# Forget attention and the last attention turn four slabs of their output in their last places instead of two, and forget attention's scores rotate over three PSUM banks

## The reference, cut to what matters

```python
def even_layer(...):
    proj = rms_norm(h, norm_g) @ w_in
    ...
    oa = rms_norm(diff_attention(...), subln_g) * (1.0 - lam_init)        # 4 heads of 128: columns 0 to 511
    ob = fox_attention(qb, kb, vb, cum_logf)                              # 4 heads of 128: columns 512 to 1023
    mixed = concatenate([oa, ob], axis=-1) * silu(z)
    return h + mixed @ w_out

def odd_layer(...):
    ...                                                                    # 8 heads of 128, three dilated windows merged
    mixed = o.reshape(b, s_len, MIX_WIDTH) * silu(z)
    return h + mixed @ w_out
```

## Time and profile before

| | |
|---|---|
| runs of the kernel before | 1555.58, 1555.17, 1554.95 us; median 1555.17 |
| the profiled execution | 1554.78 us, its span 1553.0 us |
| TensorE busy | 1487.5 us, 96% of the span |
| VectorE, ScalarE, GpSimd busy | 850.9, 677.9 and 592.3 us |
| mean granted TensorE clock | 0.998 |

### The profile page before, as it was taken

How to read it: one execution, slowest core, us unless ns; L and a number is a source line. 1 busy time by engine, 2 the same in 40 slices (tenths; PEclk the granted TensorE clock), 3 DMA queues, 4 the chain that set the end, 5 groups by cost and what they waited for, 6 DMA issues and landing times.

```text
span 1553.0 us, 25078 instructions
## 1 busy us (share of the span) xinstructions
PE 1487.5 (96%) x9488; PEld 1240.5 (80%) x9488; DVE 850.9 (55%) x1879; ACT 677.9 (44%) x1377; POOL 592.3 (38%) x349
## 2 busy tenths in 40 slices
PE   4999998898999999999899999999999999999998
PEld 3778787787888878888788889967788788877887
DVE  4573708876764265933742997056322599617322
ACT  3333336565566353335744333467323433346332
POOL 1212223691005553447725444423234444430244
PEclk9999999999999999999999999999999999999999
DMA  9657620000012333331013323300233233310322
GB/s 326 181 140 192 175 62 27 2 2 1 2 35 89 108 109 96 95 95 42 28 33 94 96 82 98 93 14 28 69 93 106 75 99 101 96 41 1 109 82 95
DMA packets 103717, 128.61 MB, mean 83 GB/s; under 512 B 10608, under 2 KB 63792, under 8 KB 103600
## 3 DMA queue, kind: packets, MB, share of 16 engines
q1 hardware_dynamic: 103600, 127.01, 27.4%
HBM read 124.90 MB, written 2.10 MB: 82 GB/s over the span
## 4 chain that ended last, share of the span: by engine, by line
PE 81%; DVE 7%; POOL 5%; ACT 3%; issue 3%; DMA 1%; SPq 1%; DVEq 0%; ACTq 0%; POOLq 0%
PE psum L1048 21%; PE psum L1050 20%; PE psum L1049 20%; PE psum L1293 3%; PE psum L1236 3%; PE psum L1004 2%; PE psum L1215 2%; PE psum L1151 1%; PE psum L1340 1%; PE psum L1322 1%; PE psum L1272 1%; POOL rx L2403 1%; POOL mla_q L2403 1%; DVE psum L1943 1%; PE psum L1273 1%
## 5 line engine op out<-in xcount | busy, mean ns | idle before, releaser
L2353 POOL TENSOR_TENSOR wlo<-wraw,whi 128x1024 fp32r<-128x1024 f32 (+4 forms) x181 | 413.1, 2283 | 704.6 <-ACT whi L1445 704.6
L1445 ACT ACTIVATE whi<-wraw 128x1024 fp32r<-128x1024 f32 (+4 forms) x181 | 181.6, 1003 | 421.7 <-PE psum L1050 415.4
L1048 PE MATMUL psum<-whi,h2h 128*128 128x512 f32 (+2 forms) x800 | 309.5, 387 | 2.6 <-DVE h2l L1959 1.5
L1050 PE MATMUL psum<-whi,h2l 128*128 128x512 f32 (+2 forms) x800 | 305.2, 382 | 0.0
L1049 PE MATMUL psum<-wlo,h2h 128*128 128x512 f32 (+2 forms) x800 | 304.6, 381 | 0.0
L1048 PEld LDWEIGHTS psum<-whi,h2h 128*128 128x128 f32 x800 | 150.3, 188 | 28.5 <-issue 2.7
L1050 PEld LDWEIGHTS psum<-whi,h2l 128*128 128x128 f32 x800 | 150.2, 188 | 27.1
L1049 PEld LDWEIGHTS psum<-wlo,h2h 128*128 128x128 f32 x800 | 150.4, 188 | 24.8
L1048 PE MATMUL psum<-whi,hTh 128*128 128x512 f32 (+2 forms) x372 | 143.4, 385 | 3.7 <-DVE hTl L1959 2.7
L1050 PE MATMUL psum<-whi,hTl 128*128 128x512 f32 (+2 forms) x372 | 136.2, 366 | 0.0
L1049 PE MATMUL psum<-wlo,hTh 128*128 128x512 f32 (+2 forms) x372 | 135.8, 365 | 0.0
(11 more groups left out here) (391 smaller groups left out, 2956.4 us busy)
## 6 DMA issues: line engine op xcount, KB each, us to landing
rx<-mod_w_in SPq DMA_DIRECT2D x32, 512.0 KB, 5.1
wraw<-w_in_odd_in SPq DMA_DIRECT2D x32, 512.0 KB, 3.6
wraw<-cd_w_in_in SPq DMA_DIRECT2D x24, 512.0 KB, 3.7
wraw<-w_in_even_in SPq DMA_DIRECT2D x20, 512.0 KB, 3.7
wraw<-ab_w_out_in SPq DMA_DIRECT2D x16, 512.0 KB, 3.7
wraw<-w_ple_gate_in SPq DMA_DIRECT2D x16, 512.0 KB, 3.8
mod_w_even<-mod_w_in SPq DMA_DIRECT2D x8, 512.0 KB, 10.3
wraw<-ab_w_in_in SPq DMA_DIRECT2D x8, 512.0 KB, 8.3
```

What stands on the lines that cost most here:

```text
L1048: eng.matmul(dst, a[0], ww[0], start=first, stop=False)
L1050: mm = eng.matmul(dst, a[1], ww[0], start=False, stop=last_)
L1445: eng.activation(hi_of(u)[:, :, 0:w], wraw[:, u["id"] % RAW, :, 0:w], ACT.Copy).then_inc(*to("split_hi", u["id"]))
L2353: eng.tensor_tensor(lo_of(u)[:, :, 0:w], wraw[:, u["id"] % RAW, :, 0:w], f32(hi_of(u)[:, :, 0:w]), ALU.subtract)\
```

## The change

Five edits:

- `late_turn` turns slabs 0 to 3, in places 27 to 30 of the pair pipeline and in places 27 to 30 of the odd attention. It was slabs 0 and 1 in the last two of these.
- `turns_at` turns slabs 4 and 5 beside unit 0 of `out3` and `out4` and slabs 6 and 7 beside unit 1. It was 2 and 3, 4 and 5, 6 and 7 beside units 0, 1 and 2.
- The four early slabs go through bank 7.
- Fox keeps its probabilities in slabs 4 to 7 of `both_low` (which lies over `h2l`), not 2 to 5, so that the low parts of slabs 2 and 3 can be written.
- Fox's scores go into banks 0, 2, 3 by n mod 3. Diff keeps its banks: its last place, 15, uses banks 2 and 3. Fox's first place, 16, now uses bank 2 (16 mod 3 = 1), place 17 bank 3, place 18 bank 0.

```diff
-        for name, t_ in (("in2", "h2"), ("out3", "m3"), ("out4", "m4")):
-            for u in range(-1 if t_[0] == "h" else 0, 3):
-                turns_at[name, 0, u] = [(t_, 2 * u + 2, 2 * u + 4, XT) if t_ == "h2" else (t_, 2 * u + 2, 2 * u + 4)]
+        for u in range(-1, 3):
+            turns_at["in2", 0, u] = [("h2", 2 * u + 2, 2 * u + 4, XT)]
+        for name, t_ in (("out3", "m3"), ("out4", "m4")):
+            for u in range(2):
+                turns_at[name, 0, u] = [(t_, 2 * u + 4, 2 * u + 6)]
...
-        late_turns = {"fox": "m3", "odd": "m4"}
+        late_turns, EARLY_SLABS = {"fox": "m3", "odd": "m4"}, 4
...
-            groups = groups_of(late_turns[name], 0, 2)
+            groups = groups_of(late_turns[name], 0, EARLY_SLABS)
             n_ = j - (len(units_of(name)) - 1 - len(groups))
...
-                    if name[0] == "m" and k < 2:
+                    if name[0] == "m" and k < EARLY_SLABS:
                         bank_of[name, k, g[0]] = 7
...
             if PAIR[n_][0] == "fox":
-                return both_low[:, 2 + n_ % 4, a:b]
+                return both_low[:, 4 + n_ % 4, a:b]
...
+        def pair_scores(n_):
+
+            return 2 * (n_ % 2) if PAIR[n_][0] == "diff" else (0, 2, 3)[n_ % 3]
...
-                        s0, cols = score_bank(n_), slice(t * P, (t + 1) * P)
+                        s0, cols = pair_scores(n_), slice(t * P, (t + 1) * P)
```

More of the change, by code:

```diff
@@ L1687, in pair_attention @@
                             eng.wait_ge(*at("nmax", (name, j, m)))
-                            eng.activation(pair_probs(n_, m, 0, w), psum[:, score_bank(n_) + m, 0:w], ACT.Exp, bias=nmax[:, c_:c_ + 1], scale=-1.0,
+                            eng.activation(pair_probs(n_, m, 0, w), psum[:, pair_scores(n_) + m, 0:w], ACT.Exp, bias=nmax[:, c_:c_ + 1], scale=-1.0,
                                            accum_out=rsum[:, c_:c_ + 1]).then_inc(*to("exps", (name, j, m)))
@@ L2044, in pair_attention @@
                         for m in range(2 if name == "diff" else 1):
-                            c_, sc = pair_column(n_, m), psum[:, score_bank(n_) + m, 0:w]
+                            c_, sc = pair_column(n_, m), psum[:, pair_scores(n_) + m, 0:w]
                             eng.wait_ge(*at("scores", (name, j, m)))
```

## The result

| | before | changed |
|---|---|---|
| median | 1555.11 us (6 runs, 1554.83 to 1555.97) | 1560.51 us (6 runs, 1558.31 to 1561.49) |
| the traced execution | 1554.78 us, span 1553.0 | 1559.28 us, span 1557.5 |

The ratio of the means is 1.0032, 95% interval 1.0019 to 1.0045: slower by 0.3%. The changed kernel also scatters more: its six runs span 3.2 us, those of before 1.1. The mean granted clock of its runs is 0.995 to 0.999.

The account below looks back on a forecast made before the run. TensorE, busy 1487.5 of 1553.0 us, was taken as the bound. Fox and `out3` summed to +2.04, odd and `out4` to +0.81: +2.85, 1557.63 for a profiled execution, median 0.39 higher, so 1558.0 us; range 1554.6 to 1560.2.

Parts of the forecast that it names:

- stall at place 16: Start of fox: scores now in bank 2 wait for place 15's first softmax, starting 1060.69 instead of 1058.64: +2.05 us.
- clock behind it: Rival: after 3.0 us idle at place 16 the granted clock drops to 1.2 GHz, 1.7 us more; chance 0.20.
- place 24: Fox: the scores' wait for place 22's exponential goes, because of the third bank: -0.74 us.
- wait for the norm: Fox, place 27: slab 0's turning waits for GpSimd's last norm, which moves with the stall at place 16: +1.77 us.
- `out3`, unit 1: `out3`: unit 1 no longer waits for slab 3's low part, and no successor to the stall is found: -1.50 us.
- turnings in fox, with the two moved out of `out3`: Fox: a 0.24 us wait for bank 7, plus 0.22 for two slabs turned in attention: together +0.46.
- odd and `out4`: Odd attention: 0.22 us for two moved turnings and 0.59 for waits on bank 7, `out4` unchanged: +0.81 us.
- The clock falls at the seam: Rival, diff to fox at place 16: clock falls after 3.0 us idle, 1.7 us on top, 1559.7 us; chance 0.20.
- the forecast for that case: Rival: place 16's added stall is absorbed, TensorE waits 1.87 us for the norm: 1556.1; chance 0.15 for seam or norm absorbed.
- the two terms of 0.22: Fox and odd: two slabs each, turned in attention at 0.46 us instead of 0.35 beside a product: +0.22 each.
- the 2.10 us for a bank: Early turnings through bank 7: 2.10 us from a turning's start until a matmul may use its result or bank.
- the 0.59 forecast for their waits: Odd attention: turnings wait for bank 7, 0.18 us at place 28 and 0.41 at place 29: +0.59.

Follow-up runs that it names:

- the last experiment: Against the kernel of before: fox's scores rotate from bank 0 at place 16; slabs 4, 5, 0, 1 turned early in fox, two in odd: 1552.67 us, ratio 0.9983.
- the mended kernel: The whole change, but fox's bank rotation starts at place 16 with bank 0: 1556.75 us, ratio 1.0010 to before; measured again 1554.91 (one run) and 1555.81.
- the first filling: The changed kernel plus 16 transposes of the identity into bank 6 ahead of place 16's scores: 1560.74 us, ratio 1.0032 to before.
- the filled norm's wait: The whole change with fox's rotation started from bank 0, plus 14 identity transposes into bank 7 ahead of slab 0's turning: 1555.29 us, ratio 0.9998 to before.

## Why the prediction was right or wrong, point by point

The direction was right; the size was off by 2.5 us, 1558.0 forecast and 1560.5 measured. The range went up to 1560.2, which is 0.32% above 1555.17, and the ratio measured is 1.0032: the result lies at its very end. The steps, by starts in the changed kernel's trace:

| step | forecast | measured |
|---|---|---|
| stall at place 16 | +2.05 | (1061.47 - 1057.86) - (1058.64 - 1057.07) = +2.04 |
| clock behind it | rival, +1.7 | +1.63 |
| place 24 | -0.74 | -0.91 |
| wait for the norm | +1.77 | (1088.91 - 1079.89) - (1082.57 - 1075.75) = +2.20; the second difference is the same stretch without a wait, in the last experiment |
| `out3`, unit 1 | -1.50 | 0.35 - 2.10 = -1.75 |
| turnings in fox, with the two moved out of `out3` | +0.46 | about +0.2 |
| odd and `out4` | +0.81 | +0.37 |

The sum is +3.8. The rest of the 4.5 us between the two spans lies ahead of the change: place 15's last step starts 0.79 us later (1057.07 and 1057.86), where the program is the same. It arises near 30 us, where the changed kernel's trace is already 0.88 us behind (last section).

**The step that failed is the one that took the clock for unchanged.** "The clock falls at the seam" had its place, its price and its cause right, and only 0.20 of the chance. The trace of before had shown the fall after 2.71 us of idle time; the sum itself gave 3.0 for the seam, and I set it aside because what came before the two gaps was different. The runs show the fall: the banks alone were 3.6 us slower, 1.6 us of it at the lower clock. The section of the Trainium skill that the prediction names ("TensorE: Matmul & The Clock Gate", "HAM oscillation — how this bites in real kernels") tells of bursts of matmuls that begin at the low clock behind a wait. All three traces that hold 3.00 or 3.55 us of unfilled waiting here agree. And I asked that question at one of the two new waits only. The second, for the norm, was priced at 1.77 and left there; in 12 of the mended kernel's 20 runs 1.6 to 3.0 us more were lost, and with the wait filled in none of 11. That would also explain why the changed kernel's median is above its own traced run, which caught the first fall and not the second; no trace shows it. Without the clock the steps sum to about +2.2, and the forecast was +2.85, so the other errors happened to bring the forecast 0.7 us nearer to what was measured.

**The mechanisms without the clock were right.** The stall's size and releaser, the norm that moves with the stall, what was won at place 24 given back at the norm (a wait of 1.07 us with the slabs alone, 2.05 in the mended kernel), no successor to `out3`'s stall: each is in the rows. The mended kernel's lowest runs, at 1555.1, are where 1.87 us of waiting for the norm (2.05 measured) meets what the change wins; the forecast for that case was 1556.1.

**Other terms were mis-sized.** The gains of 0.74 and 1.50 were read from the brackets, which begin at a row's modelled end; by starts they are 0.91 and 1.75. The wait for the norm, 1.77 in the sum, was 2.20 by starts; 0.17 of the difference is the larger gain at place 24, which is given back there. A turning beside a product doesn't cost 0.35 but nearly the 0.46 of the attention: the product's second matmul starts 0.31 us after its first, where others take 0.23. So the two terms of 0.22 were next to nothing. In the changed kernel the turnings of places 28, 29 and 30 follow one another after 2.11 and 2.13 us in fox and in odd, which bears out the 2.10 us for a bank; but in odd they took the place of waits that the trace of before had hidden in steps without a bracket: the 0.59 forecast for their waits came to about 0.4, and odd lost 0.37, not 0.81.

## What to carry to other kernels

Where a rotation of buffers starts in the middle of a pipeline, check its first turns against what the stage before holds, entry by entry: here the phase of the rotation decided between about 1 us won (by the rows, 0.91) and 3.6 us lost. Price a new wait of TensorE by what the clock may do behind it, and at each new wait by itself, since the three microseconds at the seam cost 1.6 more. Work that is brought forward is worth choosing by when its inputs are ready: with the rotation mended, the kernel took 1556.75 us with slabs that wait for the norm first in fox's four places, and 1552.67 with slabs that wait for nothing first (about 0.4 us of that is the odd attention, left as before).

## What the runs showed that I had not expected

- At 2.05 us of idle time the clock's fall seems to be a matter of chance: one program has three levels of run time, 1555.1, 1556.7 and about 1557.8. With 3.00 or 3.55 us of it unfilled a fall was seen in every trace, and in that of the first filling the clock fell about 1.1 us into the transposes that followed 2.17 us of idle time. The three traces of the mended kernel all caught the lowest level, so a trace can miss what the median shows.
- The kernel of before has two levels too, about 1555.1 and 1556.2, and the traces show where the difference lies. Behind the idle stretch that ends near 25 us TensorE is at half its pace in all 14 traces: 0.43 us from one matmul to the next, and 0.23 later. What differs is how long that lasts. In the kernel of before and then in the changed kernel:

```profile
28.65 0.68 PE L1048 MATMUL psum<-whi,hTh 128*128 128x512 f32 x1
29.17 0.39 PE L1049 MATMUL psum<-wlo,hTh 128*128 128x512 f32 x1
29.39 0.40 PE L1050 MATMUL psum<-whi,hTl 128*128 128x512 f32 x1
```

```profile
29.51 0.63 PE L1055 MATMUL psum<-wlo,hTh 128*128 128x512 f32 x1
29.94 0.63 PE L1056 MATMUL psum<-whi,hTl 128*128 128x512 f32 x1
...
30.73 0.40 PE L1055 MATMUL psum<-wlo,hTh 128*128 128x512 f32 x1
30.96 0.40 PE L1056 MATMUL psum<-whi,hTl 128*128 128x512 f32 x1
```

- The row of `mod_w_odd` that follows starts between 30.63 and 30.93 in eight traces, and between 31.51 and 32.13 in the other six, the changed kernel's and that of the filled norm's wait (1556.43) among them. The 1.1 us between the levels fit this. By an estimate from these numbers, the mended kernel's highest level, 2.7 us over its lowest, would be 1.6 for a fall behind the norm's wait and 1.1 for this; no trace was of that level.
- PEclk can miss a fall: from 26 to 30 us it reads 1.00 in eight of the 14 traces (in the changed kernel's too), though the matmuls there run at half their pace. The steps between matmuls tell the clock more surely.
